# A decoder trunk in split fp32: how the first three weight units and x arrive and are split

## The chip, the cores and the metric

One core of a Trainium2 chip runs the program. Its engines work beside one another and meet through semaphores: TensorE (matrix products), VectorE, ScalarE, GpSimd, and SyncE, which issues transfers. The metric is the device time of the program in microseconds (us), the median of several runs.

## What is computed

x is 256 tokens by 1024 channels in float32. Two layers change it in place of the residual:

```python
x += 0.5 * FFN1(norm(x))      # h @ (1024 x 5632), silu(gate) * up, @ (2816 x 1024)
x += mixer(norm(x))           # layer 0: sliding-window attention, layer 1: gated DeltaNet
x += 0.5 * FFN2(norm(x))
```

and a last RMS norm gives the output. The norm is x * rsqrt(mean(x*x)+eps) * w. All weights are float32 and are read once, about 173 MB in all.

## The kernel before

**Split products.** Each float32 operand is split into a high part (rounded to the type that TensorE takes at full rate, fp32r) and a low part, the rest. A product is three matmuls into one PSUM bank: hi x hi, hi x lo, lo x hi (`products`, lines 1302 to 1304; the stationary operand is the transposed activation, 128 x 128, the moving one a weight tile of 128 x 512).

**Weight units.** All weights pass in units of 128 x 2048 float32 (1 MB) through a ring of four slots: w_raw (what the transfers write), w_hi (ScalarE copies w_raw into it with rounding), w_lo (VectorE subtracts w_hi from w_raw). SP issues two transfers of 512 KB for each unit, in the order in which TensorE uses the units; slot u % 4 is loaded again once unit u has been split. A gate/up unit holds half of the contraction (four blocks of 128 channels) for 256 gate and 256 up columns: block j is columns j*512 to (j+1)*512 of the unit. Two such units, kh = 0 and 1, make a chunk of the FFN's 2816 hidden columns; eleven chunks follow one another. For each unit `in_unit` goes through token tile 0 with blocks j = 0 to 3, then tile 1: 24 matmuls a unit, 48 a chunk.

**Entering a phase.** The activation has to stand transposed (xT_hi, xT_lo, channels on partitions). `enter(e, n)` has TensorE transpose one quarter of x (one token tile, one half of the channels, four blocks) into a bank. ScalarE's `enter_hi` reads it, multiplies by the norm's weight column (norm_cols) and writes xT_hi; VectorE's `enter_lo` writes xT_lo. The order of the four quarters is `quarters(e)`. The row's rsqrt is applied later, behind the matmuls, by way of rstd (ScalarE squares x into ssq, VectorE takes the mean, ScalarE the root).

**The start (e = 0).** SP issues x tile 0 (512 KB), the three norm-weight rows (24 KB in all, into h_row), unit 0, x tile 1, then units 1, 2, 3. ScalarE issues one transfer, the conv rows. TensorE transposes the norm rows, ScalarE copies them to norm_cols, and TensorE transposes both halves of x tile 0 (`enter(0, 0)`, `enter(0, 1)`). When the whole of unit 0 has landed, ScalarE splits it in four pieces (line 706), with the xT_hi of quarter 0 behind the first piece; VectorE follows with its pieces (line 1028) and xT_lo. TensorE runs block 0 of unit 0 once both are ready, transposes tile 1's quarters behind blocks 2 and 3 of tile 0, and so on. ScalarE's and VectorE's order after that is in `ffn` with f == 0 and in `enter` on VectorE: quarter 1, unit 1, quarters 2 and 3, unit 2. After the first chunk, TensorE transposes the conv rows (line 1409) and goes on to the looped chunks, for which ScalarE's `gate_chunk` computes silu, splits unit u+4 and u+5, and evacuates the transposed hidden rows (line 1370 transposes them).

The order on each engine is the order of the code: an instruction that waits holds back all behind it on its engine.

Of the kernel before, what the change touches and what calls it, by code (L numbers as in the profile page):

```python
# [15 lines left out]
ALU = mybir.AluOpType  # L16
# [7 lines left out]
P = 128  # L24
# [9 lines left out]
UNIT = 2048  # L34
RING = 4

HQ, HKV, DH = 16, 4, 64
# [46 lines left out]
def quarters(e):  # L84

    if e in (0, E_GDN, 6):
        return [(t, half) for t in range(TT) for half in range(2)]  # L90
    return [(t, half) for half in range(2) for t in range(TT)]
# [63 lines left out]
def build(nc, x, positions, ffn1_norm, ffn1_w_gate_up, ffn1_w_down, mix_norm, ffn2_norm,  # L155
# [3 lines left out]
    with ctx:  # L159
# [101 lines left out]
        bank = [ctx.enter_context(nc.psum_tensor(f"bank{i}", [P, BANK], F32)) for i in range(8)]  # L261
        ENTER_BANKS = [4, 2]
        ACC = [(6, 7), (0, 1)]
        GATE_UP = [(6, 7), (0, 1), (2, 3)]
# [5 lines left out]

        raw_loaded = [sem(f"raw_loaded{i}") for i in range(RING)]
        first_hi = sem("first_hi")
        first_split = sem("first_split")
        hi_ready = sem("hi_ready")
        split_ready = sem("split_ready")
        pool_split = sem("pool_split")
        unit_done = sem("unit_done")

        x_loaded = [sem(f"x_loaded{t}") for t in range(TT)]
        rows_loaded = sem("rows_loaded")  # L280
# [127 lines left out]
        def raw_wait(u0, i):  # L408

            return 32 * (u0 // RING + 1) + 32 * i  # L410

        @block.sync
        def _(sp):
# [28 lines left out]
            def ffn(f, w_gu, w_down):  # L442
                u = U_FFN[f]
                for kh in range(2):
                    gate_up(u + kh, 0, w_gu, kh, 0)

                def two_chunks(i):
                    for c in range(2):
                        for kh in range(2):
                            gate_up(u + 2 + 2 * c + kh, i, w_gu, kh, 2 * i + 1 + c)  # L450
# [5 lines left out]
            def load_x(t):  # L456
                sp.dma_start(x_sb[:, t, :], x[0, t * P:(t + 1) * P, :]).then_inc(x_loaded[t], 16)
# [157 lines left out]
        def _(act):  # L615
            def split_hi(u0, i=0):
# [84 lines left out]
            act.activation(norm_cols[:], bank[0][:, 0:NORM_ROWS], ACT.Copy).then_inc(cols_ready, 1)  # L701
# [210 lines left out]
        def _(dve):  # L912
# [8 lines left out]
            def split_lo(u0, i=0):  # L921
# [53 lines left out]
            def enter(e, factor, scaled=False):  # L975
# [12 lines left out]
                else:  # L988
                    if e:
                        for n in range(3):  # L990
                            residual(e, n, factor)
                        enter_lo(e, 0)
                    enter_lo(e, 1)
                    if e:
                        residual(e, 3, factor)
                    else:
                        split_lo(1)
                    enter_lo(e, 2)
                    enter_lo(e, 3)
                    split_lo(PHASE_UNIT[e] + 2)  # L1000
                    inverse_rms(TT * (e + 1))
# [20 lines left out]
            for j in range(4):  # L1022
                at = slice(j * BANK, (j + 1) * BANK)
                if j < 3:
                    dve.wait_ge(first_hi, j + 1)
                else:
                    dve.wait_ge(hi_ready, 1)
                dve.tensor_tensor(w_lo[0][:, at], w_raw[0][:, at], w_hi[0][:, at].bitcast(F32),
                                  ALU.subtract).then_inc(first_split if j < 3 else split_ready, 1)
                if j == 0:  # L1030
                    enter_lo(0, 0)
            ffn(0, None)
# [266 lines left out]
        def _(pe):  # L1299
# [13 lines left out]
            def enter(e, n):  # L1313
# [3 lines left out]
                if e == 0:  # L1317
                    pe.wait_ge(x_loaded[t], 16)
                elif e == E_GDN:
# [3 lines left out]
                for j in range(4):  # L1323
                    kt = 4 * half + j
                    dst = bank[ENTER_BANKS[t] + half][:, j * P:(j + 1) * P]
                    src = x_sb[:, t, kt * P:(kt + 1) * P]
# [6 lines left out]
            def in_unit(u0, i, kh, banks, e=None):  # L1333


                if u0 or looped(i):
                    wait_split(pe, u0, i)
                for t in range(TT):
                    if e is not None:
                        pe.wait_ge(xT_lo_ready, 4 * e + quarters(e).index((t, kh)) + 1)  # L1340
                    for j in range(4):
                        if u0 == 0 and not looped(i) and t == 0:
                            if j < 3:
                                pe.wait_ge(first_split, j + 1)
                            else:
# [81 lines left out]
            pe.wait_ge(rows_loaded, 16 * 3)  # L1427
            pe.transpose(bank[0][:, 0:NORM_ROWS], norm_rows, ident[0:NORM_ROWS, 0:NORM_ROWS]).then_inc(cols_psum, 1)
            for n in range(2):
                enter(0, n)  # L1430
            ffn(0, E_ATT)
# [316 lines left out]
```

## Time and profile before

| | |
|---|---|
| median of three runs | 1110.52 us (1110.36 to 1112.6) |
| the profiled execution, its own time | 1110.62 us |
| its span in the trace | 1108.6 us |
| TensorE matmul busy | 1067.3 us, 96% |
| VectorE busy | 610.6 us, 55% |
| ScalarE busy | 529.7 us, 48% |
| mean rate of transfers over the span | 158 GB/s |

Matmuls are pipelined: a 128x512 matmul shows 0.39 us in a row but the next one starts 0.23 us after it. Times of rows below are from the start of the span. In the timeline a row is: start, duration, engine, line, operation, output tile and inputs, count, and in brackets the idle time of the engine before it with what ended it. SPq and ACTq are instructions that issue transfers; a transfer lands some microseconds after its issue.

### The profile page before, as it was taken

To read this page: it belongs to the slowest core of one execution; us is meant where nothing else is said; L and a number is where in the kernel's file an instruction comes from. 1 tells how busy PE (TensorE), PEld (TensorE's weight loads), DVE (VectorE), ACT (ScalarE), POOL (GpSimd) and SP (SyncE) were. 2 spreads that over 40 slices of the span, in tenths; PEclk is the share of its full clock that TensorE was granted. 3 is DMA by queue.
4 is the path that set the end of the run, shared out by engine and by line. 5 is a ranking of instruction groups with operands and counts; after the bars stand their busy time and mean duration, and the time that the engine had idled before them with its cause. 6 is when DMAs were issued, how large, how long until landed. Compare 5 with 4: busy or idle time off the path is not lost.

```text
span 1108.6 us, 14578 instructions
## 1 busy us (share of the span) xinstructions
PE 1067.3 (96%) x5480; PEld 900.1 (81%) x5480; DVE 610.6 (55%) x823; ACT 529.7 (48%) x772; POOL 106.1 (10%) x117
## 2 busy tenths in 40 slices
PE   6999999987999999999999998999998999999997
PEld 4888888865788888888888887989997988888885
DVE  5555554568565456446454645583596455545542
ACT  6535343455564354336443435582476346344431
POOL 0000000142000000000000004540333100000000
PEclk9999999999999999999999999998998999999999
DMA  8665565431345645645646553420341065465520
GB/s 302 193 201 179 191 226 188 147 131 39 111 157 189 210 168 199 218 152 170 209 154 224 189 191 118 153 77 1 113 152 41 3 226 170 156 215 191 217 93 38
DMA packets 123310, 174.68 MB, mean 158 GB/s; under 512 B 7152, under 2 KB 97536, under 8 KB 123264
## 3 DMA queue, kind: packets, MB, share of 16 engines
q1 hardware_dynamic: 120832, 172.01, 45.6%
q10 hardware_dynamic: 2432, 2.03, 0.6%
q8 instruction: 31, 0.51, 0.2%
q14 instruction: 15, 0.12, 0.0%
HBM read 172.98 MB, written 1.05 MB: 157 GB/s over the span
## 4 chain that ended last, share of the span: by engine, by line
PE 87%; DVE 7%; ACT 3%; POOL 1%; issue 1%; DMA 1%; ACTq 0%; SPq 0%; DVEq 0%; POOLq 0%
PE bank L1302 25%; PE bank L1304 25%; PE bank L1303 25%; PE bank L1593 4%; PE bank L1370 2%; PE bank L1564 1%; PE bank L1587 1%; DVE w_lo L924 1%; PE bank L1678 1%; PE bank L1330 1%; DVE prob L1098 1%; DVE X L1221 1%; ACT y_sb L624 1%; DMA w_raw<-in_ffn_w_gate_up 1%; ACT w_hi L621 0%
## 5 line engine op out<-in xcount | busy, mean ns | idle before, releaser
L924 DVE TENSOR_TENSOR w_lo<-w_raw,w_hi 128x2048 fp32r<-128x2048 f32 x153 | 365.1, 2391 | 153.7 <-ACT w_hi L621 153.4
L621 ACT ACTIVATE w_hi<-w_raw 128x2048 fp32r<-128x2048 f32 x161 | 307.8, 1919 | 116.0 <-PE bank L1304 115.5
L1302 PE MATMUL bank<-w_hi,xT_hi 128*128 128x512 f32 x784 | 313.3, 400 | 6.6 <-DVE xT_lo L944 5.3
L1304 PE MATMUL bank<-w_hi,xT_lo 128*128 128x512 f32 x784 | 306.7, 391 | 0.0
L1303 PE MATMUL bank<-w_lo,xT_hi 128*128 128x512 f32 x784 | 306.1, 390 | 0.0
L1302 PEld LDWEIGHTS bank<-w_hi,xT_hi 128*128 128x128 f32 x784 | 147.7, 188 | 38.8 <-DVE xT_lo L944 5.9
L1304 PEld LDWEIGHTS bank<-w_hi,xT_lo 128*128 128x128 f32 x784 | 147.6, 188 | 31.7
L1303 PEld LDWEIGHTS bank<-w_lo,xT_hi 128*128 128x128 f32 x784 | 147.9, 189 | 29.9 <-issue 0.7
L655 ACT ACTIVATE silu_g<-bank,rstd 128x256 f32<-128x256 f32 x88 | 37.0, 471 | 250.1 <-PE bank L1304 250.1
L1302 PE MATMUL bank<-w_hi,hT_hi 128*128 128x512 f32 x352 | 138.1, 392 | 0.0
L1304 PE MATMUL bank<-w_hi,hT_lo 128*128 128x512 f32 x352 | 137.1, 390 | 0.0
L1303 PE MATMUL bank<-w_lo,hT_hi 128*128 128x512 f32 x352 | 137.0, 389 | 0.0
L967 DVE SCALAR_TENSOR_TENSOR h_row<-bank,rstd,silu_g 128x256 f32<-128x256 f32 x88 | 38.5, 479 | 164.3 <-ACT silu_g L655 164.2
L1304 PEld LDWEIGHTS bank<-w_hi,hT_lo 128*128 128x128 f32 x352 | 66.1, 188 | 13.9
L1303 PEld LDWEIGHTS bank<-w_lo,hT_hi 128*128 128x128 f32 x352 | 66.1, 188 | 13.3
L1302 PEld LDWEIGHTS bank<-w_hi,hT_hi 128*128 128x128 f32 x352 | 66.1, 188 | 13.3
L1302 PE MATMUL bank<-xT_hi,w_hi 128*128 128x256 f32 x192 | 54.8, 285 | 1.9 <-DVE xT_lo L944 1.9
L1304 PE MATMUL bank<-xT_hi,w_lo 128*128 128x256 f32 x192 | 54.3, 283 | 0.0
L1303 PE MATMUL bank<-xT_lo,w_hi 128*128 128x256 f32 x192 | 54.3, 283 | 0.0
L579 POOL TENSOR_TENSOR w_lo<-w_raw,w_hi 128x2048 fp32r<-128x2048 f32 x8 | 40.2, 5031 | 98.4 <-ACT w_hi L621 98.4
L637 ACT ACTIVATE xT_hi<-bank,norm_cols 128x128 fp32r<-128x128 f32 x96 | 27.0, 377 | 32.5 <-PE bank L1330 32.5
L547 POOL MEMSET wba_hi<- 128x1024 f32 x1 | 1.0, 961 | 419.9 <-PE bank L1304 419.9
(265 smaller groups left out, 1094.7 us busy)
## 6 DMA issues: line engine op xcount, KB each, us to landing
w_raw<-in_ffn_w_gate_up SPq DMA_DIRECT2D x176, 512.0 KB, 4.7
w_raw<-in_ffn_w_down SPq DMA_DIRECT2D x88, 512.0 KB, 4.0
w_raw<-in_gdn_w_in SPq DMA_DIRECT2D x32, 512.0 KB, 4.5
w_raw<-in_attn_w_in SPq DMA_DIRECT2D x12, 512.0 KB, 4.3
w_raw<-in_attn_w_out SPq DMA_DIRECT2D x8, 512.0 KB, 4.3
w_raw<-in_gdn_w_out SPq DMA_DIRECT2D x8, 512.0 KB, 5.5
x_sb<-in_x SPq DMA_DIRECT2D x2, 512.0 KB, 5.1
out<-y_sb SPq DMA_DIRECT2D x4, 256.0 KB, 2.1
```

Source lines behind the costliest of these rows:

```text
L579: pool.tensor_tensor(w_lo[u % RING][:], w_raw[u % RING][:], w_hi[u % RING][:].bitcast(F32), ALU.subtract).then_inc(pool_split, 1)
L621: act.activation(w_hi[u0 % RING][:], w_raw[u0 % RING][:], ACT.Copy).then_inc(hi_ready, 1)
L624: act.activation(junk, src, ACT.Square, accum_out=ssq[:, t:t + 1]).then_inc(ssq_ready, 1)
L637: z = act.activation(xT_hi[:, kt, t * P:(t + 1) * P], bank[ENTER_BANKS[t] + half][:, j * P:(j + 1) * P], ACT.Copy, scale=norm_cols[:, norm ...
L655: act.activation(silu_g[j % 2][:, t, :], bank[gu_banks(j)[t]][:, 0:FC], ACT.Silu, scale=rstd[:, t:t + 1]).then_inc(silu_ready, 1)
L924: dve.tensor_tensor(w_lo[u0 % RING][:], w_raw[u0 % RING][:], w_hi[u0 % RING][:].bitcast(F32), ALU.subtract).then_inc(split_ready, 1)
L967: dve.scalar_tensor_tensor(h_row[j % 2][:, t, :], bank[gu_banks(j)[t]][:, FC:2 * FC], rstd[:, t:t + 1], silu_g[j % 2][:, t, :], ALU.mult, ...
L1302: pe.matmul(out_ap, a[0], b[0], start=start, stop=False, **kw)
L1303: pe.matmul(out_ap, a[0], b[1], start=False, stop=False, **kw)
L1304: return pe.matmul(out_ap, a[1], b[0], start=False, stop=stop, **kw)
L1370: z = pe.transpose(bank[4 + j % 2][:, k * SEQ + t * P:k * SEQ + (t + 1) * P], h_row[j % 2][:, t, k * P:(k + 1) * P], ident[:])
L1593: z = pe.matmul(bank[to][:, h * P // 2:(h + 1) * P // 2].rearrange("p (n b) -> p n b", b=b), a[:, h, :], block_columns(m[:, h, :], b, odd) ...
```

## The change

SP's issue order and sizes for x and for units 0, 1, 2 change: x arrives in four pieces of 256 KB (each a tile and a half of the channels), each of the units in four pieces of 256 KB (one block each) with a semaphore for each piece. The norm rows are issued by ScalarE, ahead of the conv rows. The order of the quarters for e = 0 becomes the same as that of most phases, half outer. Of x only quarter 0 is transposed ahead of the first matmul, each of its four blocks into a bank of its own; quarters 1, 2 and 3 are transposed behind blocks 0, 2 and 3 of tile 0 of unit 0. ScalarE and VectorE take turns, block by block, between a block of xT and a block of unit 0; units 1 and 2 are split by blocks as well (`parts_hi`, `parts_lo`), and TensorE waits for each block. The norm columns' bank is 7 instead of 0.

```diff
+FIRST = 3
-    if e in (0, E_GDN, 6):
+    if e in (E_GDN, 6):
         return [(t, half) for t in range(TT) for half in range(2)]
     return [(t, half) for half in range(2) for t in range(TT)]
+        FIRST_BANKS = [4, 0, 1, 3]
...
-            return 32 * (u0 // RING + 1) + 32 * i
+            return 32 * (u0 // RING + (0 if u0 % RING < FIRST else 1)) + 32 * i
...
-                if u0 == 0:
-                    load_x(1)
+            def first_part(u0, j):
+                v = ffn1_w_gate_up[0].rearrange("(h t p) (g c n) -> h t c p g n", h=2, t=4, p=P, g=2, c=NCH)
+                sp.dma_start(w_raw[u0][:, j * BANK:(j + 1) * BANK].rearrange("p (g n) -> p g n", g=2),
+                             v[u0 % 2, j, u0 // 2]).then_inc(part_loaded[u0][j], 16)
...
-            load_x(0)
-            for n, w in enumerate([ffn1_norm, mix_norm, ffn2_norm]):
-                sp.dma_start(norm_rows[n * 2 * KT:(n + 1) * 2 * KT, :],
-                             w.rearrange("l (t p) -> (l t) p", p=P)).then_inc(rows_loaded, 16)
+            load_x(0, 0)
+            first_part(0, 0)
+            first_part(0, 1)
+            load_x(1, 0)
+            first_part(0, 2)
+            first_part(0, 3)
+            load_x(0, 1)
+            first_part(1, 0)
+            first_part(1, 1)
+            load_x(1, 1)
+            first_part(1, 2)
+            first_part(1, 3)
+            for j in range(4):
+                first_part(2, j)
...
+            def parts_hi(u0):
+                for j in range(4):
+                    act.wait_ge(part_loaded[u0][j], 16)
+                    at = slice(j * BANK, (j + 1) * BANK)
+                    act.activation(w_hi[u0][:, at], w_raw[u0][:, at], ACT.Copy).then_inc(
+                        part_hi if j < 3 else hi_ready, 1)
...
-                    enter_hi(e, range(1, 2))
-                    split_hi(1)
-                    enter_hi(e, range(2, 4))
-                    split_hi(2)
+                    enter_hi(e, range(1, 3))
+                    parts_hi(1)
+                    enter_hi(e, range(3, 4))
+                    parts_hi(2)
...
+            for n, w in enumerate([ffn1_norm, mix_norm, ffn2_norm]):
+                act.dma_start(norm_rows[n * 2 * KT:(n + 1) * 2 * KT, :],
+                              w.rearrange("l (t p) -> (l t) p", p=P)).then_inc(rows_loaded, 16)
...
-            act.wait_ge(raw_loaded[0], raw_wait(0, 0))
+            act.wait_ge(xT_psum, 1)
             for j in range(4):
+                act.activation(xT_hi[:, j, 0:P], bank[FIRST_BANKS[j]][:, 0:P], ACT.Copy,
+                               scale=norm_cols[:, norm_col(0, j):norm_col(0, j) + 1]).then_inc(
+                                   first_hi if j < 3 else xT_hi_ready, 1)
+                act.wait_ge(part_loaded[0][j], 16)
                 at = slice(j * BANK, (j + 1) * BANK)
                 act.activation(w_hi[0][:, at], w_raw[0][:, at], ACT.Copy).then_inc(first_hi if j < 3 else hi_ready, 1)
-                if j == 0:
-                    enter_hi(0, range(1))
...
+            def parts_lo(u0):
+                for j in range(4):
+                    at = slice(j * BANK, (j + 1) * BANK)
+                    if j < 3:
+                        dve.wait_ge(part_hi, 3 * (u0 - 1) + j + 1)
+                    else:
+                        dve.wait_ge(hi_ready, u0 + 1)
+                    dve.tensor_tensor(w_lo[u0][:, at], w_raw[u0][:, at], w_hi[u0][:, at].bitcast(F32),
+                                      ALU.subtract).then_inc(part_split if j < 3 else split_ready, 1)
...
-                    enter_lo(e, 1)
-                    if e:
+                        enter_lo(e, 1)
                         residual(e, 3, factor)
+                        enter_lo(e, 2)
+                        enter_lo(e, 3)
+                        split_lo(PHASE_UNIT[e] + 2)
                     else:
-                        split_lo(1)
-                    enter_lo(e, 2)
-                    enter_lo(e, 3)
-                    split_lo(PHASE_UNIT[e] + 2)
+                    else:
+                        enter_lo(e, 1)
+                        enter_lo(e, 2)
+                        parts_lo(1)
+                        enter_lo(e, 3)
+                        parts_lo(2)
...
+                    dve.wait_ge(xT_hi_ready, 1)
+                z = dve.scalar_tensor_tensor(xT_lo[:, j, 0:P], bank[FIRST_BANKS[j]][:, 0:P],
+                                             norm_cols[:, norm_col(0, j):norm_col(0, j) + 1],
+                                             xT_hi[:, j, 0:P].bitcast(F32), ALU.mult, ALU.subtract)
...
-                        if e == 0 and kh == 0 and t == 0 and j >= 2:
-                            enter(e, j)
+                        if e == 0 and kh == 0 and t == 0 and j != 1:
+                            enter(e, max(j, 1))
...
-            for n in range(2):
-                enter(0, n)
+            enter(0, 0)
```

## Rows read from the trace of the kernel before

**Rows 1.** The page, busy time of the engines: us, share, instructions.
```profile
PE 1067.3 (96%) x5480; PEld 900.1 (81%) x5480; DVE 610.6 (55%) x823; ACT 529.7 (48%) x772; POOL 106.1 (10%) x117
```

**Rows 2.** Waits of TensorE: total us, times, longest us.
```profile
PE bank L1302 <- DVE xT_lo L944: 7.1, 3, 4.0
PE bank L1428 <- DMA h_row<-in_ffn_norm: 5.5, 1, 5.5
```

**Rows 3.** Chain of waits, 0 to 60 us: start, us, what.
```profile
8.82 0.63 ACT w_hi L706
10.51 1.14 DVE xT_lo L944 x4
...
12.48 0.43 PE bank L1303
...
19.51 0.23 PE bank L1303
...
38.50 0.44 PE bank L1370 x4
```

**Rows 4.** Timeline of TensorE, 0 to 45 us.
```profile
5.73 1.97 PE L1330 MATMUL bank<-ident,x_sb 128*128 128x128 f32 x8
...
11.69 0.79 PE L1302 MATMUL bank<-w_hi,xT_hi 128*128 128x512 f32 x1 [3.99 <-DVE xT_lo L944]
...
16.37 0.48 PE L1302 MATMUL bank<-w_hi,xT_hi 128*128 128x512 f32 x1
...
17.15 0.60 PE L1330 MATMUL bank<-ident,x_sb 128*128 128x128 f32 x4
...
19.01 0.50 PE L1302 MATMUL bank<-w_hi,xT_hi 128*128 128x512 f32 x1 [1.26 <-DVE xT_lo L944]
...
27.30 0.25 PE L1409 MATMUL bank<-ident,h_row 96*128 96x96 f32 x1
```

**Rows 5.** The same timeline, ScalarE and VectorE.
```profile
9.35 1.12 ACT L637 ACTIVATE xT_hi<-bank,norm_cols 128x128 fp32r<-128x128 f32 x4
...
10.35 1.68 ACT L706 ACTIVATE w_hi<-w_raw 128x512 fp32r<-128x512 f32 x3
...
11.55 1.89 DVE L1028 TENSOR_TENSOR w_lo<-w_raw,w_hi 128x512 fp32r<-128x512 f32 x3
...
20.61 1.07 ACT L624 ACTIVATE y_sb<-x_sb 128x1024 f32<-128x1024 f32 x1
...
22.68 1.93 ACT L621 ACTIVATE w_hi<-w_raw 128x2048 fp32r<-128x2048 f32 x1
...
24.63 1.28 ACT L628 ACT_TABLE_LOAD   x1
...
31.52 4.49 DVE L924 TENSOR_TENSOR w_lo<-w_raw,w_hi 128x2048 fp32r<-128x2048 f32 x2 [1.22 <-ACT w_hi L621]
```

**Rows 6.** The same timeline, SP's issues of the norm rows.
```profile
1.71 0.41 SPq L461 DMA_DIRECT2D h_row<-in_mix_norm  x1
2.16 0.42 SPq L461 DMA_DIRECT2D h_row<-in_ffn_norm  x1
```

**Rows 7.** Issue to landing: tiles h_row (start), pos_i (all), x_sb (start).
```profile
DMA to landing us min/median/max: 3.2/3.4/3.7
...
DMA to landing us min/median/max: 5.5/5.5/5.5
...
DMA to landing us min/median/max: 3.9/5.1/6.3
```

**Rows 8.** Windows: stretch, length, busy of engines, granted clock, DMA share, GB/s.
```profile
2.00:3.00 1.00, 0.00 (x0) 0.00 (x0) 0.00 (x0) 0.53 (x1) 0.00 (x0) 1.00 0.44 143
...
9.00:12.00 3.00, 0.31 (x1) 0.31 (x2) 2.18 (x6) 3.00 (x9) 0.00 (x0) 1.00 1.07 382
258.70:262.10 3.40, 3.40 (x16) 3.00 (x15) 3.40 (x3) 1.23 (x3) 2.79 (x2) 0.50 0.00 0
750.20:760.40 10.20, 9.24 (x44) 8.94 (x44) 2.92 (x6) 3.85 (x11) 0.00 (x0) 0.50 0.00 0
```

More of the change, by code:

```diff
@@ L271, in build @@
         raw_loaded = [sem(f"raw_loaded{i}") for i in range(RING)]
+        part_loaded = [[sem(f"part_loaded{u}_{j}") for j in range(4)] for u in range(FIRST)]
         first_hi = sem("first_hi")
         first_split = sem("first_split")
+        part_hi = sem("part_hi")
+        part_split = sem("part_split")
         hi_ready = sem("hi_ready")
@@ L277, in build @@
         unit_done = sem("unit_done")
-        x_loaded = [sem(f"x_loaded{t}") for t in range(TT)]
+        x_loaded = [[sem(f"x_loaded{t}_{half}") for half in range(2)] for t in range(TT)]
         rows_loaded = sem("rows_loaded")
@@ L443, in ffn @@
                 u = U_FFN[f]
-                for kh in range(2):
-                    gate_up(u + kh, 0, w_gu, kh, 0)
+                if f:
+                    for kh in range(2):
+                        gate_up(u + kh, 0, w_gu, kh, 0)
                 def two_chunks(i):
@@ L449, in two_chunks @@
                         for kh in range(2):
-                            gate_up(u + 2 + 2 * c + kh, i, w_gu, kh, 2 * i + 1 + c)
+                            if u + 2 + 2 * c + kh >= FIRST or looped(i):
+                                gate_up(u + 2 + 2 * c + kh, i, w_gu, kh, 2 * i + 1 + c)
                 rounds(sp, f, two_chunks)
@@ L454, in ffn, with load_x @@
                     rows(u + GU_UNITS + d, w_down, d)
-            def load_x(t):
-                sp.dma_start(x_sb[:, t, :], x[0, t * P:(t + 1) * P, :]).then_inc(x_loaded[t], 16)
-            load_x(0)
-            for n, w in enumerate([ffn1_norm, mix_norm, ffn2_norm]):
-                sp.dma_start(norm_rows[n * 2 * KT:(n + 1) * 2 * KT, :],
-                             w.rearrange("l (t p) -> (l t) p", p=P)).then_inc(rows_loaded, 16)
+            def load_x(t, half):
+                at = slice(half * BANK, (half + 1) * BANK)
+                sp.dma_start(x_sb[:, t, at], x[0, t * P:(t + 1) * P, at]).then_inc(x_loaded[t][half], 16)
+            load_x(0, 0)
[12 more added lines that the diff above has]
+                first_part(2, j)
             ffn(0, ffn1_w_gate_up[0], ffn1_w_down[0])
@@ L1024, in _ @@
                 if j < 3:
-                    dve.wait_ge(first_hi, j + 1)
+                    dve.wait_ge(first_hi, 2 * j + 1)
                 else:
+                    dve.wait_ge(xT_hi_ready, 1)
+                z = dve.scalar_tensor_tensor(xT_lo[:, j, 0:P], bank[FIRST_BANKS[j]][:, 0:P],
+                                             norm_cols[:, norm_col(0, j):norm_col(0, j) + 1],
+                                             xT_hi[:, j, 0:P].bitcast(F32), ALU.mult, ALU.subtract)
+                if j < 3:
+                    dve.wait_ge(first_hi, 2 * j + 2)
+                else:
+                    z.then_inc(xT_lo_ready, 1)
                     dve.wait_ge(hi_ready, 1)
@@ L1029, in _ @@
                                   ALU.subtract).then_inc(first_split if j < 3 else split_ready, 1)
-                if j == 0:
-                    enter_lo(0, 0)
             ffn(0, None)
@@ L1317, in enter @@
                 if e == 0:
-                    pe.wait_ge(x_loaded[t], 16)
+                    pe.wait_ge(x_loaded[t][half], 16)
                 elif e == E_GDN:
@@ L1324, in enter @@
                     kt = 4 * half + j
-                    dst = bank[ENTER_BANKS[t] + half][:, j * P:(j + 1) * P]
+                    if e == 0 and n == 0:
+                        dst = bank[FIRST_BANKS[j]][:, 0:P]
+                    else:
+                        dst = bank[ENTER_BANKS[t] + half][:, j * P:(j + 1) * P]
                     src = x_sb[:, t, kt * P:(kt + 1) * P]
@@ L1333, in in_unit @@
             def in_unit(u0, i, kh, banks, e=None):
-                if u0 or looped(i):
+                by_parts = u0 < FIRST and not looped(i)
+                if not by_parts:
                     wait_split(pe, u0, i)
                 for t in range(TT):
-                    if e is not None:
+                    if e is not None and (e or kh or t):
                         pe.wait_ge(xT_lo_ready, 4 * e + quarters(e).index((t, kh)) + 1)
                     for j in range(4):
-                        if u0 == 0 and not looped(i) and t == 0:
-                            if j < 3:
+                        if by_parts and t == 0:
+                            if j < 3 and u0 == 0:
                                 pe.wait_ge(first_split, j + 1)
+                            elif j < 3:
+                                pe.wait_ge(part_split, 3 * (u0 - 1) + j + 1)
                             else:
@@ L1427, in _ @@
             pe.wait_ge(rows_loaded, 16 * 3)
-            pe.transpose(bank[0][:, 0:NORM_ROWS], norm_rows, ident[0:NORM_ROWS, 0:NORM_ROWS]).then_inc(cols_psum, 1)
-            for n in range(2):
-                enter(0, n)
+            pe.transpose(bank[7][:, 0:NORM_ROWS], norm_rows, ident[0:NORM_ROWS, 0:NORM_ROWS]).then_inc(cols_psum, 1)
+            enter(0, 0)
             ffn(0, E_ATT)
```

2 lines of the change are left out of this document (1 added, 1 removed).

## The prediction

> **What bounds the kernel now.** I read the engine totals first: TensorE is busy 96% of the span [rows 1], so what can be won is idle TensorE time and slow TensorE time. Then its waits: 7.1 us on xT_lo in three places and 5.5 us on the norm rows stand near the top [rows 2]. The timeline puts 5.49 us of the second and two of the first (4.0 and 1.26 us, of 7.1) ahead of 19.1 us [rows 4]. The same timeline shows the first matmul of unit 0 at 11.69, a hole of 1.26 us ahead of 19.01, and the end of chunk 0 (units 0 and 1, both token tiles) at 27.30, where the conv transposes start. The chain of waits tells what made 11.69: the first weight unit, landed as two 512 KB transfers, freed ScalarE at 8.82; a quarter of w_hi, four xT_hi and four xT_lo follow, up to 11.65 [rows 3]. From 27.30 to 60 no row of the timeline has TensorE idle, and it has the ring's splits in time from there, so what comes off 27.30 should come off the end. The sum therefore is: when does chunk 0 end?
>
> Two levels of TensorE's clock are in that stretch. A 512-column matmul takes 0.43 us of the chain at 12.48 and 0.23 at 19.51 [rows 3]: 1.2 and 2.4 GHz. The low level lasts up to 16.3, 4.65 us behind the first matmul; ahead of it TensorE had only done nine transposes from 5.49 to 7.7 [rows 4]. (The clock column reads 1.00 there, as it starts with the first recorded change.) In chunk 0 there are 2 units x 2 tiles x 4 x 3 = 48 matmuls, 48 x 0.2275 = 10.92 at the high level; a group of four x transposes adds about 0.55 (0.60 at 17.15, less overlap). Before: 11.69 + 10.92 + 2 x 0.55 + half of the low stretch 2.33 + hole 1.26 = 27.3, which is what the trace has.
>
> **The head.** The norm rows' three transfers move from SP's queue, behind x, to ScalarE's, ahead of the conv rows: issued about 0.80, 1.25, 1.71, where SP had the third at 2.16 (0.45 a piece [rows 6]). Landing took 3.2 to 3.7 us for h_row's four transfers [rows 7]; 3.7 is the conv rows, the only one on ScalarE's queue, so I take that: 1.71 + 3.7 = 5.4. The bounds are 3.2 (4.9) and the 5.5 of pos_i, issued by ScalarE beside running weight loads [rows 7] (7.2). ScalarE issues four transfers instead of one: 1.35 more, then its table load 1.28, done near 3.95, hidden by the wait for the rows. On TensorE, norm transpose and then only four x transposes instead of eight: 0.24 + 1.97/2 = 1.25 [rows 4], so 6.65. ScalarE: xT_hi 0.28 (1.12/4), w_hi quarter 0.63; VectorE: w_lo quarter 0.63; handovers 0.2 [rows 3, 5]. First matmul at 8.4 to 8.5: take 8.45, 3.25 sooner.
>
> Is data there? Transfers are issued every 0.45 us, 256 KB each: faster than the 382 GB/s at which they run once several are queued [rows 8], that is 0.69 us for a quarter. The start is slower (143 GB/s from 2 to 3 us [rows 8]), x's first 512 KB landed 3.9 us behind its issue [rows 7]. I put x's first quarter at 4.3, unit 0's at 4.9, 5.6, 7.0, 7.7, the other x quarters at 6.3, 8.4 and 10.5, unit 1's at 9.1, 9.8, 11.1, 11.8. ScalarE wants unit 0's at 6.9, 7.7, 8.5, 9.3. Everything has over a microsecond of cover. Taking turns costs xT_hi 0.28 and w_hi 0.56 for each quarter on ScalarE, and xT_lo 0.28 and w_lo 0.63 on VectorE [rows 5]: 0.91 per quarter, against 1.28 for TensorE's three matmuls at the low level. So from 8.45 on TensorE is the one that sets the pace.
>
> **The hole at 19.0.** The old order is (tile, half), so tile 1 was transposed only behind the third and fourth quarter of unit 0, and its xT_hi and xT_lo came after the splitting of unit 1 (xT_lo from 17.83), while TensorE stood. By the new order (half outer) tile 1's first half is transposed behind the first three matmuls, and xT_hi and xT_lo for it follow the initial four quarters: done by 12.9, wanted at 15.0. The hole goes, 1.26. One group of four transposes more now lies in the stream (three, was two): 0.55 back. What is late next? Walking it with the low level up to 13.1: matmuls of quarters 0 to 3 end at 9.7, 11.9, 13.2, 14.4, tile 1 at 17.7. ScalarE stands still from 11.8 to 13.8 for the third group of transposes, then xT_hi to 15.0, unit 1's quarters to 17.2, the last xT_hi to 18.4, unit 2's to 20.6. VectorE: xT_lo to 16.2, w_lo of unit 1 at 16.9, 17.5, 18.1, 18.7, last xT_lo 19.9. TensorE wants them at 17.7, 18.4, 19.1, 19.8 and 20.5. The cover is 0.6 to 1.1 us: thin, but there.
>
> **Behind chunk 0.** Splitting by quarters costs 4 x 0.56 against one whole 1.93, and 4 x 0.63 against 2.29: 0.3 us a unit on either engine, for units 1 and 2, hidden as just walked. Then ScalarE: two squares of 1.07, unit 3 in 1.93, root and silu with a table load of 1.28 each, unit 4 [rows 5]: w_hi done at 30.1 and w_lo at 32.4. TensorE wants unit 4 behind chunk 1's two units and chunk 0's h transposes, at 23.4 + 0.25 + 10.9 + 0.4 = 35.0. Before it was ready at 33.8 (31.52 and half of 4.49 [rows 5]) for 38.9 (h transposes from 38.50 [rows 3]); 5.1 of cover become about 2.6. Extra waits in TensorE's stream (one for each quarter of units 1 and 2) are on semaphores long set: nothing, at most 8 x 0.05. SP's 16 first issues are done by 8.0 at 0.45 each; unit 3 follows, and unit 4 waits as before for unit 0's split, now at 11, long before ScalarE wants it at 28.
>
> **The sum.** 8.45 + 10.92 + 3 x 0.55 + 2.33 = 23.35 against 27.30: 3.25 + 1.26 - 0.55 = 3.95 sooner. The profiled execution took 1110.62 (span 1108.6 and 2.0 around it), 0.1 above the median 1110.52: 1106.7, and 1106.6 as a median.
>
> The low clock's length is the largest unknown, as every microsecond of it costs half of one. Rows elsewhere in the trace have low stretches of 3.4 and of 10.2 us with TensorE at work [rows 8]: 0.6 better, 2.8 worse. I keep 4.65, the row of the same place. The Trainium skill, "TensorE: Matmul & The Clock Gate" (What's actually happening), says that one kernel shows different numbers of slow matmuls from run to run, with where its first matmul falls; one trace can't show that, and by it my 2.33 would be one draw of several.
>
> **Rivals.**
> (a) The norm rows land late: ScalarE's queue shares the engines with 256 KB pieces already under way. pos_i's 5.5 speaks for it, the conv rows' 3.7, beside x, against. At 5.5 the first matmul is 1.8 later: 1108.4.
> (b) The low clock lasts 10.2 us. The thinner, earlier start (five transposes, then a break to 8.45) is for it; that TensorE is then without a break is against. 1106.6 + 2.8 = 1109.4.
> (c) A new wait takes the hole's place: ScalarE stands for the third group of transposes, and unit 1's split or the last xT_lo is over a microsecond late. Cover 0.6; each engine's walk would have to be 1.7 us short: 1107.7.
> (d) Slower than before: the quarters don't run at 382 GB/s but at the rate seen when little is queued, 143 [rows 8]. The last quarter of unit 1 is byte 3.15 MB of the queue: 1.9 + 22.0 + 1.0 to land = 24.9; its split 1.3, three matmuls 0.7, tile 1 2.7 give 29.6 for 27.3: 1112.8. It decides from about 160 GB/s downwards. Against it: from 9 us on, with several transfers queued and the same 1 KB runs, the trace holds 382 [rows 8], and here three are queued by 1.7.
> The Trainium skill, "DMA: Bandwidth & Descriptors", Bandwidth, speaks for (d): it wants transfers batched to 1 MiB or more for three quarters of peak. By its fit of 2.0 us plus the bytes over 436 GB/s, a quarter is 2.6 us: an estimate that would matter only if they ran one behind the other. The trace has 512 KB transfers at 382 GB/s when queued, so it does not agree for queued ones; at 256 KB no run here shows it.
>
> **Numbers.** Forecast 56% (1105.2 to 1107.6), (a) 15%, (b) 13%, (c) 10%, (d) 6%. A measurement of this kernel tells 0.2%, 2.2 us, from no change: faster means below 1108.3. The forecast, (c), and the halves of (a) and (b) with partial lateness give 0.80; the rest of these 0.14; slower 0.06. Range: 0.6 and 1.0 better (clock, rows at 3.2) to (b): 1105.0 to 1109.4.
>
> **What would show it.** Right: first L1302 near 8.4; no idle row on xT_lo in TensorE's first 25 us; conv transposes near 23.4; the matmul step falling from 0.43 to 0.23 some 4 to 5 us behind the first; the same totals from there. Norm transpose after 6.5: (a). Step still 0.43 at 16: (b). A row of TensorE waiting on w_lo or xT_lo between 17 and 21: (c). ScalarE waiting on w_raw before 17: (d). The forecast is wrong if chunk 0 ends 4 us sooner and the total does not: then a later stage gave it back, which no row of before suggests.

## The result: 5.9 us faster, where 3.9 were forecast

The changed kernel's median is 1105.13 us (seven executions, 1099.58 to 1105.64), the kernel before beside it 1111.05 (seven, 1110.36 to 1112.6): 5.9 us less. The ratio of the two kernels over all these executions is 0.9939 (it is not the quotient of the medians, which is 0.9947), 95% interval 0.9927 to 0.9952, that is 5.3 to 8.1 us less. The direction was right and the way it came was the forecast one, but the gain was half as large again. Over all executions of this study the means are 1110.65 (79 of before) and 1104.92 (18 of after): 5.7 us.

The profiled execution of the changed kernel took 1104.44, its span is 1102.6. The page comes first: its totals are within 2.3 us of those of before [rows 1].

```profile
PE 1065.1 (97%) x5480; PEld 897.8 (81%) x5480; DVE 611.2 (55%) x829; ACT 530.1 (48%) x778; POOL 106.1 (10%) x117
```

TensorE's waits, total, times, longest; they answer to [rows 2]:

```profile
PE bank L1489 <- DMA h_row<-in_ffn_norm: 4.7, 1, 4.7
...
PE bank L1357 <- DVE xT_lo L990: 1.9, 1, 1.9
...
PE bank L1357 <- DVE w_lo L1085: 1.8, 1, 1.8
...
PE bank L1357 <- DVE w_lo L959: 0.8, 1, 0.8
```

xT_lo was 7.1 us in three waits; the one of 1.9 that is left lies later in the kernel. The two at the start are gone, and 1.8 us on the first quarter of w_lo stand in their place. In the timeline of TensorE, line 1489 is the norm transpose, 1388 the x transposes, 1357 the first of the three matmuls, 1470 the conv transpose (lines 1428, 1330, 1302, 1409 before):

```profile
4.66 0.31 PE L1489 MATMUL bank<-ident,h_row 48*128 48x48 f32 x1 [4.66 <-DMA h_row<-in_ffn_norm]
...
4.91 1.12 PE L1388 MATMUL bank<-ident,x_sb 128*128 128x128 f32 x4
...
7.79 0.79 PE L1357 MATMUL bank<-w_hi,xT_hi 128*128 128x512 f32 x1 [1.77 <-DVE w_lo L1085]
...
9.24 1.05 PE L1388 MATMUL bank<-ident,x_sb 128*128 128x128 f32 x4
...
12.65 1.01 PE L1388 MATMUL bank<-ident,x_sb 128*128 128x128 f32 x4
...
13.36 0.54 PE L1357 MATMUL bank<-w_hi,xT_hi 128*128 128x512 f32 x1
...
22.84 0.25 PE L1470 MATMUL bank<-ident,h_row 96*128 96x96 f32 x1
```

From 7.79 on no row has a bracket: TensorE runs through, past 19.01 where it had stood. Against [rows 4] the first matmul is 3.90 sooner, the end of chunk 0 4.46. The chain of waits gives the matmuls' steps, 0.43 at the low clock and 0.23 at the high one, and the path through the norm rows that makes 7.79:

```profile
1.71 2.81 DMA h_row<-in_ffn_norm
4.66 0.31 PE bank L1489
4.98 1.06 PE bank L1388 x4
6.13 0.37 ACT xT_hi L738
6.49 0.53 ACT w_hi L743
7.04 0.70 DVE w_lo L1085
7.79 0.79 PE bank L1357
8.59 0.43 PE bank L1358
...
12.85 0.81 PE bank L1388 x4
13.66 0.23 PE bank L1357
...
14.37 0.44 PE bank L1388 x4
```

The spans differ by 6.0, chunk 0 by 4.46. The windows view has the rest: columns as in [rows 8]. At that place in the program (258.7 us before, around 255 now), where before 3.4 us ran at 0.50, the clock stays at 1.00 in this execution (half of 3.4 is 1.7); the stretch of some 10 us near 750 is in both:

```profile
2.00:3.00 1.00, 0.00 (x0) 0.00 (x0) 0.00 (x0) 0.34 (x1) 0.00 (x0) 1.00 0.78 273
9.00:12.00 3.00, 3.00 (x11) 2.41 (x10) 2.02 (x5) 1.85 (x6) 0.00 (x0) 1.00 1.02 337
253.00:259.00 6.00, 4.16 (x30) 3.37 (x30) 5.86 (x10) 2.93 (x11) 3.68 (x2) 1.00 0.00 0
743.90:754.20 10.30, 8.96 (x42) 8.27 (x42) 4.30 (x6) 3.17 (x8) 1.01 (x1) 0.50 0.01 2
```

A little of the gain lies outside the span. An execution's time less its span is 2.00 to 2.13 us in all 72 executions of before with a span on record beside the later kernels, 1.78 to 1.87 in the 18 of the changed kernel, and 1.74 to 1.83 in the twelve of rows_only below: some 0.25 us go with the norm rows' change of queue. What they are made of, no trace shows.

So two questions: is the part behind chunk 0 an effect of the change or the clock's draw (where in an execution the clock happens to be low, and how long), and why is chunk 0 better than the forecast?

### The profile page after: what moved, and what is told of

Same layout as the page of the kernel before. It is cut to its first block, busy times and chain, and to the rows that moved or that the text cites. A ratio compares the mean times of both kernels' runs of the same rounds, so it can differ in the third digit from the quotient of the medians.

```text
span 1102.6 us, 14592 instructions
## 1 busy us (share of the span) xinstructions
PE 1065.1 (97%) x5480; PEld 897.8 (81%) x5480; DVE 611.2 (55%) x829; ACT 530.1 (48%) x778; POOL 106.1 (10%) x117
## 3 DMA queue, kind: packets, MB, share of 16 engines
HBM read 172.98 MB, written 1.05 MB: 158 GB/s over the span
## 4 chain that ended last, share of the span: by engine, by line
PE 88%; DVE 7%; ACT 3%; POOL 1%; issue 1%; DMA 0%; ACTq 0%; DVEq 0%; POOLq 0%
PE bank L1357 25%; PE bank L1359 25%; PE bank L1358 25%; PE bank L1653 4%; PE bank L1431 2%; PE bank L1624 1%; PE bank L1647 1%; DVE w_lo L959 1%; PE bank L1388 1%; PE bank L1738 1%; DVE prob L1153 1%; DVE X L1276 1%; ACT y_sb L654 1%; ACT w_hi L643 1%; PE bank L1563 0%
## 5 line engine op out<-in xcount | busy, mean ns | idle before, releaser
L959 DVE TENSOR_TENSOR w_lo<-w_raw,w_hi 128x2048 fp32r<-128x2048 f32 x151 | 360.8, 2395 | 152.9 <-ACT w_hi L643 152.6
L643 ACT ACTIVATE w_hi<-w_raw 128x2048 fp32r<-128x2048 f32 x159 | 304.0, 1919 | 116.1 <-PE bank L1359 115.5
L1359 PEld LDWEIGHTS bank<-w_hi,xT_lo 128*128 128x128 f32 x784 | 147.6, 188 | 31.7
L1357 PEld LDWEIGHTS bank<-w_hi,hT_hi 128*128 128x128 f32 x352 | 66.1, 188 | 13.3
```

The costliest lines, as they stand in the source:

```text
L959: dve.tensor_tensor(w_lo[u0 % RING][:], w_raw[u0 % RING][:], w_hi[u0 % RING][:].bitcast(F32), ALU.subtract).then_inc(split_ready, 1)
L1357: pe.matmul(out_ap, a[0], b[0], start=start, stop=False, **kw)
L1359: return pe.matmul(out_ap, a[1], b[0], start=False, stop=stop, **kw)
```

## Experiments

Ratios are to the kernel before, run beside each of them on the same chip. Three groups of four ran together: before_again, after_again, hold4, rows_only; coarse, whole12, old_order, one_row; after_3, x_whole, w_whole, one_row_2. "Norm transpose" is TensorE's transpose of the norm rows, which starts some 0.14 us after the last of them has landed. "Low" is the time from the first 512-column matmul to the step's fall from 0.43 to 0.23; "equal" is the end of chunk 0 less half of it, which takes the clock's draw out of the start; "rest" is the span less the end of chunk 0.

| profile | norm transpose | first matmul | low | chunk 0 ends | equal | rest | median (ratio, 95%) |
|---|---|---|---|---|---|---|---|
| before | 5.49 | 11.69 | 4.65 | 27.30 | 25.0 | 1081.3 | 1111.05 |
| before_again | 5.53 | 12.14 | 4.03 | 27.45 | 25.4 | 1081.3 | 1110.31 (1.0001; 0.9992 to 1.0010) |
| after | 4.66 | 7.79 | 5.69 | 22.84 | 20.0 | 1079.8 | 1105.13 (0.9939; 0.9927 to 0.9952) |
| after_again | 4.61 | 7.74 | 3.30 | 21.65 | 20.0 | 1081.7 | 1105.02 (0.9950; 0.9938 to 0.9962) |
| after_3 | 4.80 | 7.92 | 4.57 | 22.42 | 20.1 | 1082.4 | 1106.29 (0.9957; 0.9944 to 0.9970) |
| hold4 | 8.63 | 11.76 | 4.82 | 26.39 | 24.0 | 1079.3 | 1109.47 (0.9991; 0.9982 to 1.0000) |
| rows_only | 7.35 | 11.33 | 6.12 | 27.09 | 24.0 | 1079.5 | 1109.39 (0.9986; 0.9975 to 0.9996) |
| coarse | 7.33 | 10.46 | 5.19 | 25.23 | 22.6 | 1079.5 | 1107.91 (0.9976; 0.9967 to 0.9985) |
| x_whole | 5.36 | 8.48 | 3.97 | 22.70 | 20.7 | 1082.0 | 1106.48 (0.9959; 0.9946 to 0.9972) |
| w_whole | 6.50 | 9.62 | 5.97 | 24.79 | 21.8 | 1079.9 | 1106.56 (0.9968; 0.9958 to 0.9977) |
| whole12 | 4.79 | 7.91 | 4.21 | 24.03 | 21.9 | 1080.4 | 1106.17 (0.9962; 0.9947 to 0.9977) |
| old_order | 4.79 | 7.91 | 5.83 | 24.56 | 21.6 | 1081.5 | 1107.44 (0.9970; 0.9957 to 0.9982) |
| one_row | 3.19 | 6.74 | 4.97 | 21.51 | 19.0 | 1082.4 | 1104.92 (0.9944; 0.9930 to 0.9957) |
| one_row_2 | 3.29 | 6.52 | 3.33 | 20.58 | 18.9 | 1081.8 | 1102.82 (0.9935; 0.9923 to 0.9948) |

### The same kernels again

No edit. 

> The kernel before, unchanged, to have the granted clock of each of its executions. Both theories: 1110.4 to 1112. Theory 1 (the head alone, the rest is the clock's draw): executions with more time at the low clock are longer, and a line through span against low time holds for this kernel and for the changed one, some 4.5 us apart. Theory 2 (the remainder is systematic): the low time of this kernel's executions lies clearly above that of the changed kernel's.

> The changed kernel, unchanged. Theory 1: its executions scatter from about 1099 to 1106 by the time at the low clock, and at equal low time they lie 4.5 us (the 4.46 that chunk 0 ends sooner in the profile) under the kernel before. Theory 2: 5.9 us under it or more at equal low time.

The rest behind chunk 0 was 1081.3 in both profiles of before, and 1079.8, 1081.7 and 1082.4 in three of the changed kernel: not lower as a rule. after_again had a low stretch of 3.4 us near 685 and none near 255, before_again both. The spread of the rest goes with those stretches, whatever the kernel: the five profiles that have neither (after, hold4, rows_only, coarse, w_whole) have 1079.3 to 1079.9, the nine with one or both 1080.4 to 1082.4. At equal low clock chunk 0 ends 5.0 to 5.4 sooner. Mean clocks of single executions overlap (0.986 to 0.991 for before, 0.986 to 0.991 for after_again; one of the first seven had 0.996 and took 1099.58). Compared at the same mean clock, before's executions are longer by 5.4 us (at 0.986), 5.1 (0.988, the one with most executions, 42 and 9), 5.0 (0.989) and 5.6 (0.991): 5.2 together, with a standard error of some 0.2 and with the 0.25 outside the span in it. Theory 1 holds, with a head of 5.0 to 5.4 in place of the 4.5 that one pair of profiles shows; theory 2's 5.9 or more does not. The range forecast for after_again's executions, 1099 to 1106, was too wide: 1103.74 to 1106.07.

### The whole start held back

```diff
+            for _ in range(4):
+                after(pool.memset(y_sb[:, 0, :], 0.0))
+            pool.memset(y_sb[:, 1, 0:8], 0.0).then_inc(hold, 1)
...
+            sp.wait_ge(hold, 1)
             load_x(0, 0)
...
+            act.wait_ge(hold, 1)
```

> The changed kernel with its whole start held back by four GpSimd memsets of some 1.1 us each in a row (first transfers of SyncE and ScalarE wait for them), so that every stage lies about 4.5 us later, where it lay before the change. Theory 1 (head alone): the changed kernel's time plus the held time, about 1105.1 + 4.5 = 1109.6, a little under the kernel before. Theory 2 (where the later stages lie in time matters): the whole 5.9 us come back, 1111 or more.

The first transfer went out at 4.96 for 0.80, so the hold is 4.16 us, not 4.5:

```profile
4.96 0.39 SPq L470 DMA_DIRECT2D x_sb<-in_x  x1
```

The mean of its twelve executions is 1109.23, 4.3 over the changed kernel's 1104.92; its median 1109.47. Theory 1 wanted 4.2, theory 2 some 5.7. The first matmul, at 11.76, and the end of chunk 0 at equal clock lay 4.0 us later, near where they had been before, and only 4.3 us came back: nothing that these times resolve rests on where the later stages lie.

### The norm rows alone

```diff
-            for n, w in enumerate([ffn1_norm, mix_norm, ffn2_norm]):
-                sp.dma_start(norm_rows[...], ...)
...
+            for n, w in enumerate([ffn1_norm, mix_norm, ffn2_norm]):
+                act.dma_start(norm_rows[...], ...)
             act.dma_start(conv_rows, ...)
```

> The kernel before, with only the three norm rows issued by ScalarE ahead of the conv rows (one part of the change alone). My walk: the first weight unit is issued 1.4 us sooner (1.25 for 2.62), lands 1 to 1.4 sooner, first matmul near 10.5 for 11.69, the hole at tile 1 stays: 1.0 to 1.4 us faster, about 1110.0 (1109.5 to 1110.3). The rival that the head is bound by bytes and not by issue: under 0.3 us.

0.9 us faster by the medians, at 1109.39 a little under the expected range, but less of it in the head than walked. Issued 0.45 us sooner, the third row landed 1.8 later, at 7.2. The first matmul came at 11.33 where 10.5 was expected, 0.4 to 0.8 sooner than before, since unit 0 landed sooner (ScalarE starts on it at 8.45, for 8.82 and 9.27), and the hole shows 0.72:

```profile
1.71 0.51 ACTq L696 DMA_DIRECT2D h_row<-in_ffn_norm  x1
...
7.35 0.31 PE L1428 MATMUL bank<-ident,h_row 48*128 48x48 f32 x1 [7.35 <-DMA h_row<-in_ffn_norm]
...
8.45 0.63 ACT L706 ACTIVATE w_hi<-w_raw 128x512 fp32r<-128x512 f32 x1 [0.54 <-DMA w_raw<-in_ffn_w_gate_up]
...
11.33 0.80 PE L1302 MATMUL bank<-w_hi,xT_hi 128*128 128x512 f32 x1 [1.76 <-DVE xT_lo L944]
...
18.79 0.50 PE L1302 MATMUL bank<-w_hi,xT_hi 128*128 128x512 f32 x1 [0.72 <-DVE xT_lo L944]
```

The smaller hole is the clock's draw: the low stretch lasted 6.12 us, so TensorE came later to the place where it waits. The last microsecond of that stretch, behind the transposes that end at 16.4, was hidden in the hole. So half of the whole stretch is too much to take off here, and this profile's 24.0 in the table is too good by about 0.5, an estimate: at equal low clock its chunk 0 ends 0.4 to 0.9 sooner. With the 0.25 outside the span that is 0.7 to 1.1, as the medians have it.

The late row is rival (a) of the prediction, in a kernel where the transfers beside the rows are of 512 KB. In the changed kernel the same third row, issued at the same 1.71, landed in 2.8 us. The next three say which transfers hold it up.

### The size of the transfers

coarse has both of these edits, x_whole the first, w_whole the second (a unit's split then waits for the whole unit):

```diff
-                sp.dma_start(x_sb[:, t, at], x[0, t * P:(t + 1) * P, at]).then_inc(x_loaded[t][half], 16)
+                if half == 0:
+                    sp.dma_start(x_sb[:, t, :], x[0, t * P:(t + 1) * P, :]).then_inc(x_loaded[t][0], 16)
...
-                sp.dma_start(w_raw[u0][:, j * BANK:(j + 1) * BANK].rearrange("p (g n) -> p g n", g=2),
-                             v[u0 % 2, j, u0 // 2]).then_inc(part_loaded[u0][j], 16)
+                sp.dma_start(w_raw[u0][:].rearrange("p (t g n) -> p t g n", t=4, g=2)[:, :, g, :],
+                             v[u0 % 2, g, u0 // 2]).then_inc(part_loaded[u0][0], 16)
```

> The changed kernel with the transfers of before: x in two of 512 KB, units 0 to 2 in two of 512 KB each, a unit's split waiting for the whole of it; order of engines, splitting by blocks and ScalarE's issue of the norm rows stay. Theory 1 (the size of the transfers ahead sets when the norm rows and unit 0 land; with 512 KB ones the rows, issued by ScalarE, landed only at 7.35 us): first matmul near 10.3 for 7.8, 2 to 2.5 us slower than the changed kernel, 1107.2 to 1107.6. Rival (order and turns give all, the size of transfers nothing): within 0.7 us of the changed kernel, 1105.0 to 1105.7.

> The changed kernel with x in two transfers of 512 KB and the units still in quarters. In both kernels with all transfers of 512 KB the norm rows on ScalarE's queue landed at 7.3 us. If x's large first transfer is what holds the rows up, they land near 7.3 here, first matmul near 10.4, 1107.4. If it is the units' transfers, rows near 4.7, first matmul near 7.9, 1105.2.

> The other half: x in quarters, units 0 to 2 in two transfers of 512 KB, a split waiting for the whole unit. If x's first transfer holds the rows up: rows near 4.7, unit 0 whole near 7.5 to 8, first matmul near 9.3 to 9.6, 1106.6. If the units' transfers do: rows near 7.3, first matmul near 10.4, 1107.6.

> The changed kernel once more, on the same chip and beside the three kernels below, so that they are compared with it and not only with the kernel before. Its median has been 1105.13 and 1105.02: 1104.5 to 1105.6.

The norm transpose in coarse, x_whole and w_whole, one kernel to a fence:

```profile
7.33 0.31 PE L1491 MATMUL bank<-ident,h_row 48*128 48x48 f32 x1 [7.33 <-DMA h_row<-in_ffn_norm]
```

```profile
5.36 0.31 PE L1489 MATMUL bank<-ident,h_row 48*128 48x48 f32 x1 [5.36 <-DMA h_row<-in_ffn_norm]
```

```profile
6.50 0.31 PE L1491 MATMUL bank<-ident,h_row 48*128 48x48 f32 x1 [6.50 <-DMA h_row<-in_ffn_norm]
```

Neither theory of x_whole and w_whole was right: both sizes delay the rows, x's by 0.6 to 0.7, the units' by 1.8, both together by 2.6, and nearly all of it is in the first matmul (0.6, 1.8, 2.6). That w_whole's first matmul and median meet the first theory's 9.6 and 1106.6 is chance: its rows were to be there at 4.7. coarse's theory 1 was right (10.46, 1107.91 where 1107.2 to 1107.6 were expected), and coarse is still 2.4 to 2.8 us ahead of before at equal low clock: everything but the smaller transfers (order, turns, splitting by blocks, the rows' queue) gives about one half of chunk 0's gain, the smaller transfers the other. In each of the three, unit 0's first quarter was not what was waited for: the chain runs through the rows. after_3 missed its expected 1104.5 to 1105.6, at 1106.29, with the changed kernel unedited; so much can a median of five be off.

Size is one reading. The other is how many bytes SyncE has put under way: in all four kernels it had started three transfers by 2 us, 0.79 MB in the changed kernel, 1.05 in x_whole, 1.31 in w_whole, 1.57 in coarse. At the rates below, 296 to 338 GB/s, the 0.26, 0.52 and 0.79 MB more take 0.8 to 0.9, 1.6 to 1.8 and 2.3 to 2.7 us, an estimate that meets the delays of 0.6 to 0.7, 1.8 and 2.6. No run has small transfers and many bytes, or the reverse, so the two aren't told apart. Quarters cost rate (from 1.5 to 12 us of each profile):

```profile
1.50:12.00 10.50, 5.57 (x17) 4.32 (x18) 4.21 (x10) 5.96 (x14) 0.02 (x1) 1.00 0.93 296
```

```profile
1.50:12.00 10.50, 2.90 (x9) 2.04 (x10) 2.64 (x6) 4.70 (x10) 0.02 (x1) 1.00 0.98 338
```

296 GB/s in the changed kernel (first), 338 in coarse (second), and the kernel with the slower stream is 2.6 us better. The Trainium skill's "DMA: Bandwidth & Descriptors" (Bandwidth) wants large transfers for rate; by that rule, the trace agrees in direction, 12% here, and nothing waits for the rate. The same page (Queues, rings and completion order) says that the engines take turns between ScalarE's and SyncE's queues after each packet; no run here shows the turns, and they alone do not tell 2.8 from 5.5 us for one 8 KB transfer. Where the delay arises (at the engines, or in the making of the two queues' descriptors) was not tried.

### Splits of units 1 and 2 whole

```diff
-                for j in range(4):
-                    act.wait_ge(part_loaded[u0][j], 16)
-                    ...
+                for j in range(4):
+                    act.wait_ge(part_loaded[u0][j], 16)
+                act.activation(w_hi[u0][:], w_raw[u0][:], ACT.Copy).then_inc(hi_ready, 1)
```

(VectorE's part likewise, and TensorE waits for whole units from unit 1 on.) 

> The changed kernel with units 1 and 2 split whole (one ScalarE and one VectorE instruction each), transfers still in quarters. My prediction's walk: w_lo of unit 1 is wanted in quarters from 17.4 on and would be whole only near 18.9: a hole of 1.3 to 1.6 ahead of unit 1, time 1106.3 to 1106.6. Rival (the units' splits are hidden either way): no hole, 0.1 to 0.3 faster for the engines' shorter work, 1104.9.

```profile
16.57 0.39 PE L1350 MATMUL bank<-w_hi,xT_lo 128*128 128x512 f32 x1
18.45 0.50 PE L1348 MATMUL bank<-w_hi,xT_hi 128*128 128x512 f32 x1 [1.50 <-DVE w_lo L957]
```

The hole came where it was expected, 1.50 us ahead of unit 1; at equal clock chunk 0 is 1.9 longer. From the matmul ahead of the hole to the one behind it are 1.88 us where a step is 0.23, so 1.65 are lost for the 1.50 in the bracket, and the first matmul is 0.1 later. Its five times, 1105.01 to 1108.27 with a median of 1106.17, overlap those of the changed kernel, so it is the trace that shows this one.

### The old order of quarters

```diff
-    if e in (E_GDN, 6):
+    if e in (0, E_GDN, 6):
```

(and x's second and third piece swapped in SyncE's order). 

> The changed kernel with the old order of the four quarters of x (token tile outer), x's pieces fetched in that order. My walk: xT_lo of tile 1's first half is ready near 16 where TensorE wants it between 14.4 and 15: a hole of 1 to 1.5 in front of tile 1 comes back, 1106.0 to 1106.5. Rival (the hole went by itself, since TensorE starts sooner and x is there): no hole, 1105.0.

```profile
14.39 0.60 PE L1388 MATMUL bank<-ident,x_sb 128*128 128x128 f32 x4
16.22 0.50 PE L1357 MATMUL bank<-w_hi,xT_hi 128*128 128x512 f32 x1 [1.23 <-DVE xT_lo L990]
```

In the changed kernel the same group of transposes has no hole behind it:

```profile
14.20 0.60 PE L1388 MATMUL bank<-ident,x_sb 128*128 128x128 f32 x4
14.56 0.48 PE L1357 MATMUL bank<-w_hi,xT_hi 128*128 128x512 f32 x1
```

The hole is back at 1.23 us in front of tile 1, on xT_lo as before. Chunk 0 is 1.6 longer at equal clock and the median 1107.44, past the expected 1106.5. From the transposes to the matmul behind them are 1.83 us here and 0.36 in the changed kernel: the hole costs 1.47 and not the bracket's 1.23, since the bracket counts only from the end of the row ahead, and with no hole the next row starts before that end (0.36 us behind the start of a row of 0.60). Another 0.1 is the first matmul.

### A faster version

```diff
+            act.dma_start(norm_rows[0:2 * KT, :],
+                          ffn1_norm.rearrange("l (t p) -> (l t) p", p=P)).then_inc(rows_loaded, 16)
...
+            pe.transpose(bank[7][:, 0:2 * KT], norm_rows[0:2 * KT, :], ident[0:2 * KT, 0:2 * KT]).then_inc(cols_psum, 1)
...
+                    pe.transpose(bank[5][:, CONV_ROWS:CONV_ROWS + NORM_ROWS], norm_rows,
+                                 ident[0:NORM_ROWS, 0:NORM_ROWS])
```

> A version meant to be faster than both: ScalarE issues only ffn1's norm row, TensorE transposes its 16 rows alone; the other rows and conv rows are issued by SyncE behind unit 1 and transposed with the conv rows after chunk 0. If the norm rows set the first matmul in the changed kernel, it starts 1.0 to 1.5 us sooner (near 6.5, then bound by unit 0's third quarter, landed at 8.2): 1104.0. If unit 0's landing sets it anyway: within 0.3 us, 1105.0.

> The version with ffn1's norm row alone at the start, once more. Its first profile ended chunk 0 at 21.51 with 4.97 us of low clock, 1.0 us under the changed kernel at equal low clock (19.0 for 20.0), but its five times had a median only 0.1 to 0.2 lower. Theory 1 (a microsecond of chunk 0 is a microsecond of the end): 0.7 to 1.2 us under after_3. Rival (it is given back later, by the extra transposes and the shifted transfers): within 0.3 us of after_3.

ScalarE and the first matmul in its first profile:

```profile
3.19 0.26 PE L1496 MATMUL bank<-ident,h_row 16*128 16x16 f32 x1 [3.19 <-DMA h_row<-in_ffn_norm]
```

```profile
5.33 0.63 ACT L748 ACTIVATE w_hi<-w_raw 128x512 fp32r<-128x512 f32 x1 [0.32 <-DMA w_raw<-in_ffn_w_gate_up]
...
7.96 0.63 ACT L748 ACTIVATE w_hi<-w_raw 128x512 fp32r<-128x512 f32 x1 [0.97 <-DMA w_raw<-in_ffn_w_gate_up]
```

In this profile unit 0's landing binds, by 0.32 us. In the second it doesn't: ScalarE starts on xT_hi at 4.78, behind the x transposes, and goes on to w_hi without a wait, so the chain still runs through the norm row and the x transposes. The rows set the first matmul in the changed kernel, and here the row and unit 0 come within a few tenths of one another. The third quarter, which was expected to bind next, kept ScalarE waiting (0.97 at 7.96 above, 1.44 in the second profile), but no row of TensorE waits for it. The second profile's two rows:

```profile
4.78 0.37 ACT L743 ACTIVATE xT_hi<-bank,norm_cols 128x128 fp32r<-128x128 f32 x1 [1.01 <-PE bank L1393]
5.11 0.63 ACT L748 ACTIVATE w_hi<-w_raw 128x512 fp32r<-128x512 f32 x1
```

The first matmul is 1.0 to 1.4 sooner and chunk 0 ends 1.0 to 1.2 sooner at equal clock, in both profiles. In times the two groups say different things: 1104.92 near the changed kernel's 1105.13 and 1105.02, then 1102.82 beside 1106.29, 3.5 under it where 0.7 to 1.2 was expected. Over eleven and eighteen executions the means are 1103.99 and 1104.92, 0.9 apart with a standard error of 0.6. The trace has the microsecond; the times fit it and don't prove it.

## Why the prediction was wrong, step by step

**What bounds it, and that chunk 0's end is the end's:** right. "Rest" is 1079.3 to 1082.4 in all fourteen profiles, without regard to where chunk 0 ends, and hold4 gave back what it was held by. Only the "2.0 around" the span was not the same for both kernels: it is 1.8 in the changed one, 0.25 better.

**The head: the step that failed.** Forecast 8.45, 3.25 sooner; it was 7.79, 7.74, 7.92 against 11.69 and 12.14, 3.8 to 4.4. The mis-sized term is "1.71 + 3.7 = 5.4" for the norm rows: the last landed at 4.5 to 4.7, in 2.8 to 2.9 us, and their transpose started at 4.66 in the first profile. From there to the first matmul it was 3.13, where 5.4 to 8.45 had allowed 3.05; so the landing is the whole of the miss of 0.66. I had taken the slowest of four transfers because it was the only one on ScalarE's queue; but it was also the only one of 48 KB, and in the changed kernel the conv rows took 3.8 to 4.0 and the 8 KB rows 2.2 to 2.9. The bound at 3.2 was not low enough either. The two profiles of the kernel before also start their first matmul 0.45 us apart, which one profile can't show.

**Cover of the data:** right in sum, wrong in two parts. SyncE's issue of 256 KB took 0.60 to 0.65 from the second on and not 0.45 (sixteen were done at 10.9, not 8.0), and in the first profile unit 0's third quarter landed late enough to hold ScalarE for 0.27 (8.31); TensorE, at the low clock, did not feel it, and the other two profiles of this kernel don't have the wait. From 9 to 12 us the rate was 337 where I had 382, from 2 to 3 us it was 273 where I had 143 [rows 8].

**The hole:** right in mechanism (old_order brings it back), and both of its terms were mis-sized: forecast 1.26 - 0.55 = 0.71. From first matmul to the end of chunk 0 at equal clock it was 13.3 in both profiles of before and 12.2 to 12.3 in three of after: 1.1. The hole cost 1.50: 1.86 us from the transposes at 17.15 to the matmul at 19.01 [rows 4], against 0.36 from 14.20 to 14.56 in the changed kernel. The transposes' group was charged 0.55; the chain has 0.81 at the low and 0.44 at the high clock, the second of which is what a group takes from the high-clock sum. 1.50 - 0.44 is 1.06, which is the 1.1. That the sum for before came out at 27.3 all the same was luck: 1.26 for the hole was too little by about what 2 x 0.55 was too much.

**Later cover:** right. Unit 4's w_lo is done at 31.7 (29.41 and half of 4.50), wanted behind the h transposes at 34.2: 2.6, as forecast. The walk of units 1 and 2 was right too: no wait, and with whole splits a hole of 1.5.

```profile
29.41 4.50 DVE L959 TENSOR_TENSOR w_lo<-w_raw,w_hi 128x2048 fp32r<-128x2048 f32 x2 [1.22 <-ACT w_hi L643]
```

**The low clock.** Kept at 4.65; the profiled after had 5.69, which cost 0.5, and thirteen others ran from 3.30 to 6.12. So the sum at equal clock is 3.95 forecast and 5.0 to 5.4 measured: 0.6 to 1.1 from the first matmul, 0.4 from the hole and the transposes. The 10.2 us of rival (b) never came at the start. The median of 1105.13 is at the lower end of the range of 1105.0 to 1109.4; by the ratio, from the 1110.52 that the forecast started from, it is 1103.7, below it. What the sum lacked is 0.66 for the landing of the rows, 0.36 for the hole and the transposes, and 0.25 outside the span. The range also left out the draw of the low stretches further on: it had only the start's. The Trainium skill's "TensorE: Matmul & The Clock Gate" (What's actually happening) says that the number of slow matmuls varies from run to run; by that rule, the trace agrees: 3.30 and 5.69 us for one kernel.

**Rivals.** (a) did not happen but is real with 512 KB transfers beside the rows (rows_only, coarse). (b), (c), (d) did not happen; the rate fell to 296, not below 160. The sign named for (d), ScalarE waiting on w_raw before 17, did show, for 0.27 us in one profile of three: as a sign it was too weak, since this wait of ScalarE cost TensorE nothing. The prediction's 2.6 us for a single quarter is what x's first took from issue to landing (2.6; unit 0's first two took 3.6 and 3.9). The fit behind that estimate stands in the Trainium skill, "DMA: Bandwidth & Descriptors" (Anatomy of one DMA), and is given there for transfers that GpSimd issues; these are SyncE's.

## What to carry to other kernels

At a start where everything waits for data, find the last thing that the first product needs: here it was 24 KB of norm weights, and they were late through the size or the number of bytes of other transfers, on another queue. Cut what is needed first into the pieces in which it is used, even at some loss of rate. When you price a hole, take the distance between the starts of the rows on both sides of it, less what it is without a hole; the idle time in the bracket was 0.15 to 0.24 us too small here. And before a microsecond is explained from two profiles, put the same stretch of several profiles side by side: one of this kernel's was 1.2 us off another in chunk 0 alone.

## What the runs showed of the hardware

- An 8 KB transfer on ScalarE's queue, issued at 1.71 us, took 2.8 to 2.9 us to land beside SyncE's 256 KB transfers, 5.5 us beside 512 KB ones, 3.5 with only x and 4.7 with only the weights in 512 KB. SyncE had started 0.79, 1.57, 1.05 and 1.31 MB by 2 us; which of the two counts, size or bytes, isn't shown.
- In the changed kernel SyncE took 0.39 us to issue the first transfer (256 KB) and 0.6 to 0.65 for each of the next fifteen. Their size alone does not set it: in x_whole 512 KB of x took 0.60 in the same place, in one_row an 8 KB row behind them took 0.60 and the next 0.41, while in coarse the two transfers of 512 KB at 1.25 us took 0.97 together. What sets it isn't shown.
- The granted clock falls to half at different places in executions of one kernel (near 255 and 685 us in some, not in others). The kernel before, without an edit, ranges over 4 us of 1110 (1108.45 to 1112.69 in 72 executions), of which the mean clock tells about 2: on average 1111.0 at 0.986 and 1109.2 at 0.991. The changed kernel was once 6 us off (1099.58 at a mean clock of 0.996, median 1105.13 at 0.988).
